# A hybrid attention and mixture-of-experts step: forget bias and masks kept in SBUF tables, and mask and extremum in one VectorE operation

## What is computed

```python
# positions: 16 meta tokens + 256 prompt rows; 8 samples of 16 new rows with 256 cached rows each
z = rms(h, attn_norm) @ w_in                      # split: fox q,k,v, forget logits, diff q,k,v
fq, fk = rms per head of 64; logf = log_sigmoid(ff + b_forget); dq, dk = rope(rms per half head)
c = cumsum(logf)                                  # over positions, per fox head
# group A, 8 fox heads of 64:
s = q.k * 64**-0.5 + c_q - c_k;  s = -inf where k_pos > q_pos;  o = softmax(s) @ v
# group B, 4 diff heads (q1,q2,k1,k2 of 64, v of 128), visible where chunk(k) <= chunk(q), chunks of 64:
p = softmax(q1.k1 * 64**-0.5) - lam * softmax(q2.k2 * 64**-0.5);  o = rms(p @ v) * (1 - 0.2)
h = h + concat(o_fox, o_diff) @ w_out
y = h + moe(rms(h, ffn_norm))                     # top 4 of 32 experts, clamped SwiGLU, gate_up 1024x2048, down 1024x1024
```

## Time and profile before

| | |
|---|---|
| median of 3 runs | 1306.97 us (1306.32 to 1307.01) |
| the profiled execution | 1314.02 us, its span 1312.2 us |
| TensorE busy | 1249.1 us (95%) |
| VectorE, ScalarE, GpSimd busy | 356.9, 197.6, 156.4 us |
| mean granted TensorE clock | 0.957 |
| moved by DMA | 447.05 MB, mean 341 GB/s |
| projections | about 20 to 176 us |
| prompt attention | 177 to 240 us |
| sample attention | 240 to 309 us |
| output projection and router | 309 to 370 us |
| experts | 370 to 1312 us |

### The profile page before, as it was taken

How to read it: one execution, slowest core, us unless ns; L and a number is a source line. 1 busy time by engine, 2 the same in 40 slices (tenths; PEclk the granted TensorE clock), 3 DMA queues, 4 the chain that set the end, 5 groups by cost and what they waited for, 6 DMA issues and landing times.

```text
span 1312.2 us, 16086 instructions
## 1 busy us (share of the span) xinstructions
PE 1249.1 (95%) x6081; PEld 556.6 (42%) x6082; DVE 356.9 (27%) x896; ACT 197.6 (15%) x522; POOL 156.4 (12%) x373
## 2 busy tenths in 40 slices
PE   5799999999989999999999999999999999999997
PEld 3344455664555344343434434343434434343432
DVE  3213335562332142221314222121313212121312
ACT  5111233442411010010101001010101001010100
POOL 0011310220041020202202020201202020210000
PEclk9999975699989999999999999999999999999998
DMA  7912340296049999999999999999999999999994
GB/s 275 338 41 80 117 172 1 81 323 240 22 200 428 429 427 429 429 426 430 428 429 430 427 430 430 427 430 428 429 430 427 430 429 427 430 428 428 428 427 174
DMA packets 54536, 447.05 MB, mean 341 GB/s; under 512 B 10817, under 2 KB 11090, under 8 KB 29922
## 3 DMA queue, kind: packets, MB, share of 16 engines
q1 hardware_dynamic: 54498, 446.54, 82.0%
HBM read 441.66 MB, written 4.86 MB: 340 GB/s over the span
## 4 chain that ended last, share of the span: by engine, by line
PE 65%; DMA 25%; SPq 4%; DVE 2%; POOL 1%; issue 1%; ACT 0%; DVEq 0%; POOLq 0%
DMA arena<-in_w_gate_up 24%; PE psum L1636 17%; PE psum L1604 17%; PE psum L1585 7%; PE psum L1343 6%; PE psum L1507 3%; PE psum L1651 2%; SPq L391 2%; PE psum L1619 1%; PE psum L1615 1%; PE psum L1396 1%; PE psum L1377 1%; PE psum L1426 1%; PE psum L1459 1%; SPq L407 1%
## 5 line engine op out<-in xcount | busy, mean ns | idle before, releaser
L1604 PE MATMUL psum<-arena 128*64 128x512 f32 x2048 | 450.6, 599 | 18.9 <-DMA arena<-in_w_gate_up 18.3
L1604 PEld LDWEIGHTS psum<-arena 128*64 128x64 f32 x2048 | 153.3, 138 | 314.3 <-issue 314.3
L1636 PE MATMUL psum<-arena 128*64 128x512 f32 x1024 | 224.8, 597 | 0.8 <-issue 0.2
L1250 DVE TENSOR_SCALAR arena<-psum 128x256 f32<-128x256 f32 x64 | 26.7, 418 | 432.4 <-PE psum L1604 430.6
L1636 PEld LDWEIGHTS psum<-arena 128*64 128x64 f32 x1024 | 78.8, 138 | 136.1 <-issue 134.7
L1343 PE MATMUL psum<-arena 128*128 128x512 f32 x288 | 127.3, 598 | 0.0
L872 ACT ACTIVATE arena<-arena 128x256 f32<-128x256 f32 x64 | 26.7, 418 | 630.5 <-DVE arena L1250 630.5
L1585 PEld LDWEIGHTS psum<-arena 128*128 128x128 f32 x768 | 88.6, 195 | 16.1 <-issue 16.1
L1585 PE MATMUL psum<-arena 128*128 128x128 f32 x768 | 91.6, 280 | 3.8 <-POOL arena L624 3.8
L617 POOL COPY arena<-arena 128x6 f32 (+1 forms) x16 | 3.0, 188 | 760.0 <-PE psum L1636 703.7
L1651 PE MATMUL psum<-arena 128*128 128x512 f32 x192 | 93.2, 623 | 0.0
(11 more groups left out here) (217 smaller groups left out, 848.9 us busy)
## 6 DMA issues: line engine op xcount, KB each, us to landing
arena<-in_w_gate_up SPq DMA_DIRECT2D x128, 2048.0 KB, 24.9
arena<-in_w_down SPq DMA_DIRECT2D x64, 2048.0 KB, 22.7
arena<-in_w_in SPq DMA_DIRECT2D x6, 2048.0 KB, 20.3
arena<-in_cache_fox_k SPq DMA_DIRECT2D x8, 512.0 KB, 5.7
arena<-in_cache_diff_k SPq DMA_DIRECT2D x8, 512.0 KB, 5.1
arena<-in_cache_fox_v SPq DMA_DIRECT2D x8, 512.0 KB, 5.8
arena<-in_cache_diff_v SPq DMA_DIRECT2D x8, 512.0 KB, 7.1
arena<-in_w_out SPq DMA_DIRECT2D x4, 1024.0 KB, 6.8
```

The source lines that it names most:

```text
L1604: last = mm(banks[n][half], XT[u][:, k, half], piece_slot(s[x])[:, c0:c0 + 512], start=False, stop=(k == 7), skip_group_check=True)
L1636: last = mm(banks[hf][half], actT[:, 4 * i + c, half], w, start=False, stop=(i == 1 and c == 3), skip_group_check=True)
```

## The change

- In the projections, after units 12, 13, 14 and 19, TensorE writes the bias of one pair of heads for all 272 keys to banks 0 and 1 (`keep_table`), and VectorE copies it to two tables in SBUF with the causal mask added where it belongs (`keep_bias`): `T1[p]` for query tile 1, `T0[p]` for query tile 0. GpSimd writes two tables `TD` with the chunk mask for the diff group.
- In the prompt attention the bias matmuls are gone. `maxes` is, for each head, one tensor_tensor_reduce: -(scores + table), written to `probs2` in SBUF, with the minimum of the row as its accumulator output. The exponential reads `probs2` in place, with scale -1.
- `scores(i)` waits for `maxed` in place of `exped`. VectorE's write to `probs2` waits for the transposes of step i - 3.
- The tables lie in ring slot 3. Its first load moves from behind unit 11 to b = 5 of the sample loop.

```diff
--- before.py
+++ after.py
@@ -149,6 +149,9 @@
         probs = [at(a0 + 13696 + 288 * i, 288) for i in range(3)]
         pT = [at3(a0 + 14560 + 384 * i, 3, 128) for i in range(2)]
         probs2 = [at3(5 * PIECE_W + 544 * i, 2, NKEY_P) for i in range(3)]
+        T1 = [at3(3 * PIECE_W + 544 * p, 2, NKEY_P) for p in range(4)]
+        T0 = [at3(3 * PIECE_W + 2176 + 288 * p, 2, META + P) for p in range(4)]
+        TD = [at(3 * PIECE_W + 3328, META + P), at(3 * PIECE_W + 3472, NKEY_P)]
         pT2 = [at3(5 * PIECE_W + 1632 + 768 * i, 2, 384) for i in range(2)]
         assert a0 + 15328 <= 53200
 
@@ -222,6 +225,7 @@
         s_vout = sem("s_vout")
         s_xr, s_wrt, s_bdn, s_bgu = sem("s_xr"), sem("s_wrt"), sem("s_bdn"), sem("s_bgu")
         s_bef, bs_ready = sem("s_bef"), sem("bs_ready")
+        bias_done, bias_kept, chunk_kept = sem("bias_done"), sem("bias_kept"), sem("chunk_kept")
         gates_ready, selg_ready, h_rc = sem("gates_ready"), sem("selg_ready"), sem("h_rc")
         cum_done, ncs_ready, lfT_done = sem("cum_done"), sem("ncs_ready"), sem("lfT_done")
         s_yout = sem("s_yout")
@@ -323,6 +327,14 @@
 
         def S_pair(i):
             return psum[:, 1024 * (i % 2):1024 * (i % 2 + 1)].rearrange("p (a n) -> p a n", a=2)
+
+        TABLE_AT = {12: 0, 13: 1, 14: 2, meta0 + 4: 3}
+        assert [units[u][0] for u in (11, 12)] == [3, 4]
+
+        def masked(x, a):
+            if x["g"] == 1:
+                return TD[x["qt"]]
+            return (T0, T1)[x["qt"]][x["j"]][:, a]
 
         pT_pair = psum[:, 2048:3072].rearrange("p (a n) -> p a n", a=2)
 
@@ -456,7 +468,7 @@
                             sp.dma_start(slot(s).rearrange("p (k n) -> p k n", k=2),
                                          io["w_out"][0, 2 * P * s:2 * P * (s + 1)].rearrange("(k p) n -> p k n", p=P)
                                          ).then_inc(s_wout, 16)
-                    elif bi < 5:
+                    elif bi not in (3, 5):
                         sp.dma_start(piece_slot(bi), piece_src(0, bi - LEAD)).then_inc(ring_in[bi], 16)
 
             for i in range(2):
@@ -473,8 +485,9 @@
                     sp.wait_ge(mixed, NP + 2 * (b - 4) + 2)
                     load_cache(b - 2, "v")
                     load_v3(b - 2)
-                if b == 4:
-                    sp.dma_start(piece_slot(5), piece_src(0, 5 - LEAD)).then_inc(ring_in[5], 16)
+                if b in (4, 5):
+                    s = {4: 5, 5: 3}[b]
+                    sp.dma_start(piece_slot(s), piece_src(0, s - LEAD)).then_inc(ring_in[s], 16)
             sp.wait_ge(scored, NA)
             for t in range(2):
                 sp.dma_start(y[:, t], io["x_prompt"][0, P * t:P * (t + 1), :]).then_inc(s_xr, 16)
@@ -566,6 +579,11 @@
                 nc.gpsimd.tensor_tensor(ov[:, :, 1], ov[:, :, 1], bv[:, :, 1], ALU.add).then_inc(z_out, 1)
 
             g_.wait_ge(zT_copied, upto(is_n, NU))
+            nc.gpsimd.memset(TD[0][:, 0:META], 0.0)
+            nc.gpsimd.memset(TD[1][:, 0:META + P], 0.0)
+            for qt in range(2):
+                last = nc.gpsimd.tensor_copy(TD[qt][:, META + P * qt:META + P * (qt + 1)], C["chunk"])
+            last.then_inc(chunk_kept, 1)
             for i in range(2):
                 g_.wait_ge(s_store[i], 16 * stores_on(NU, i))
             nc.gpsimd.memset(stat[:, 44:45], -0.5)
@@ -759,8 +777,8 @@
                 c = 2 * (i % 3)
                 if x["where"] == "p":
                     for a in range(2):
-                        last = nc.scalar.activation(probs2[i % 3][:, a, 0:x["nk"]], S_pair(i)[:, a, 0:x["nk"]], ACT.Exp,
-                                                    bias=stat[:, 12 + c + a:13 + c + a],
+                        last = nc.scalar.activation(probs2[i % 3][:, a, 0:x["nk"]], probs2[i % 3][:, a, 0:x["nk"]], ACT.Exp,
+                                                    scale=-1.0, bias=stat[:, 12 + c + a:13 + c + a],
                                                     accum_out=stat[:, 18 + c + a:19 + c + a])
                 else:
                     last = nc.scalar.activation(probs[i % 3][:, 0:x["nk"]], banks[i % 2][:, 0:x["nk"]], ACT.Exp,
@@ -954,6 +972,16 @@
                                                 in1=C["maps"][:, 0:1], op0=ALU.mult, op1=ALU.add))
             nc.vector.tensor_scalar(comb, comb, C["maps"][:, 0:1], None, ALU.mult).then_inc(comb_ready, 1)
 
+
+            def keep_bias(p):
+                B = S_pair(0)
+                causal = C["causal"].unsqueeze(1).to_broadcast([P, 2, P])
+                ve.wait_ge(bias_done, p + 1)
+                nc.vector.tensor_copy(T1[p][:, :, 0:META + P], B[:, :, 0:META + P])
+                nc.vector.tensor_tensor(T1[p][:, :, META + P:], B[:, :, META + P:NKEY_P], causal, ALU.add)
+                nc.vector.tensor_copy(T0[p][:, :, 0:META], B[:, :, 0:META])
+                nc.vector.tensor_tensor(T0[p][:, :, META:], B[:, :, META:META + P], causal, ALU.add
+                                        ).then_inc(bias_kept, 1)
 
             for u, (bi, kind, g, t) in enumerate(units):
                 if kind == "v":
@@ -990,6 +1018,8 @@
                 else:
                     ins.then_inc(z_scaled, 1)
                     ve.wait_ge(z_scaled, m + 1)
+                if u in TABLE_AT:
+                    keep_bias(TABLE_AT[u])
                 if m == 1:
                     ve.wait_ge(lfT_done, 1)
                     for t_ in range(4):
@@ -999,6 +1029,9 @@
                     ve.wait_ge(lf_ready, 2)
                     nc.vector.tensor_copy(lf_new[0:META], lf[0:META, 0:1].to_broadcast([META, 8, 8])).then_inc(lf_ready, 1)
 
+
+            keep_bias(3)
+            ve.wait_ge(bias_kept, 4)
 
             def kc_evac(s):
                 ve.wait_ge(kc_T, 2 * s + 1)
@@ -1015,11 +1048,16 @@
                 ve.wait_ge(scored, i + 1)
                 c = 12 + 2 * (i % 3)
                 if x["where"] == "p":
-                    S = S_pair(i)
-                    k0 = META + P * x["qt"]
-                    link(nc.vector.tensor_tensor(S[:, :, k0:k0 + P], S[:, :, k0:k0 + P],
-                                                 C[("causal", "chunk")[x["g"]]].unsqueeze(1).to_broadcast([P, 2, P]), ALU.add))
-                    out_, src = stat[:, c:c + 2], S[:, :, 0:x["nk"]]
+                    if x["g"] == 1:
+                        ve.wait_ge(chunk_kept, 1)
+                    if i >= 3:
+                        ve.wait_ge(turned, i - 2)
+                    for a in range(2):
+                        last = nc.vector.tensor_tensor_reduce(
+                            out=probs2[i % 3][:, a, 0:x["nk"]], in0=S_pair(i)[:, a, 0:x["nk"]], in1=masked(x, a),
+                            scale=-1.0, scalar=3.0e38, op0=ALU.add, op1=ALU.min, accum_out=stat[:, c + a:c + a + 1])
+                    last.then_inc(maxed, 1)
+                    return
                 else:
                     S = banks[i % 2]
                     k0 = META + PAST
@@ -1314,6 +1352,16 @@
                                                zo[upto(is_o, u) % 2][rows_of(u), P * j:P * (j + 1)],
                                                ident[rows_of(u), rows_of(u)])
                 last.then_inc(z_T, 1)
+
+            def keep_table(p):
+                pe.wait_ge(lf_ready, 3)
+                if p >= 1:
+                    pe.wait_ge(bias_kept, p)
+                for a in range(2):
+                    hs = slice(32 * a, 32 * a + 8)
+                    last = mm(S_pair(0)[:, a, 0:NKEY_P], ident[hs, 2 * p + 33 * a:2 * p + 33 * a + 1].to_broadcast([8, P]),
+                              nc_p[hs, 0:NKEY_P], start=True, stop=True)
+                last.then_inc(bias_done, 1)
 
             late = []
             for u, (bi, kind, g, t) in enumerate(units):
@@ -1351,6 +1399,8 @@
                         last = nc.tensor.transpose(banks[6][0:b, 448 + 8 * t_:456 + 8 * t_], ffl[0:8, a:a + b], ident[0:8, 0:8])
                     last.then_inc(lfT_done, 1)
 
+                if u in TABLE_AT:
+                    keep_table(TABLE_AT[u])
                 newest = u - 1 if u < meta0 else -1 if u < meta0 + 4 else meta0 if u < NU - 1 else u
                 while late and late[0] <= newest:
                     turn_z(late.pop(0))
@@ -1380,21 +1430,20 @@
 
             def scores(i):
                 x = att[i]
-                if i >= 2:
+                if i == 0:
+                    pe.wait_ge(bias_kept, 4)
+                elif NP + 2 > i >= 2:
+                    pe.wait_ge(maxed, i - 1)
+                elif i >= 2:
                     pe.wait_ge(exped, i - 1)
                 nk = x["nk"]
                 g = x["g"]
                 if x["where"] == "p":
                     q0, j = P * x["qt"], x["j"]
-                    if g == 0:
-                        for a in range(2):
-                            hs = slice(32 * a, 32 * a + 8)
-                            mm(S_pair(i)[:, a, 0:nk], ident[hs, 2 * j + 33 * a:2 * j + 33 * a + 1].to_broadcast([8, P]),
```

(3 more changed lines are left out.)

## The result

| | before | after |
|---|---|---|
| median of 13 and 13 executions | 1307.67 us | 1301.36 us |
| lowest, highest | 1302.73, 1315.54 | 1295.44, 1310.46 |
| profiled execution, its span | 1314.02, 1312.2 us | 1307.11, 1305.2 us |
| mean granted clock of that execution | 0.957 | 0.970 |

The account below looks back on a forecast made before the run. The prediction took prompt attention as bound by TensorE at half clock. Its terms, -7.5 + 2.1 + 3.4 us with the others 0, summed to -2.0 us, from a median of 1306.97 to 1305.0 us, range 1300.0 to 1310.0.

Parts of the forecast that it names:

- signs of being wrong: Waits on VectorE ahead of prompt attention's transposes, a granted clock above 0.5 there, or a sample stage as long as before.
- What bounds the kernel: Prompt attention, 176.6 to 239.7 us, is bound by TensorE at half clock (0.53 and 0.50).
- the clock comes back earlier: Rival: without the bias, prompt attention might hold full clock, giving 13 us, to 1292; chance 0.06.
- VectorE and ScalarE become the bound: Rival in prompt attention: if a fused operation takes 1.0 us, 8 to 9 us lost, 1313.5; chance 0.07.
- Term 1: Bias matmuls leave the fox steps of prompt attention, all on TensorE's path: -7.5 us.
- Term 2: Four bias products enter the projections, 2.6 us, less a 0.50 us wait for GpSimd at 139.10 that goes: +2.1 us.
- Term 3: VectorE fills the tables during the projections, where it has time, and GpSimd writes the diff masks: 0.
- Term 4: Fused mask and extremum on VectorE in prompt attention, 1.0 us against 1.16 per 272-key step, and exponentials from SBUF: 0.
- Term 5: Moved 2 MB load delays the sample attention's cache loads: waits of 2.1 us for keys, 1.3 for V rows: +3.4 us.
- the wait drops the clock: Rival in the sample attention: waits bring a second half-clock spell of 10.8 us, losing 5.4 us, 1310.4; chance 0.12.
- The sum: All terms over the whole kernel: -7.5 + 2.1 + 3.4 = -2.0 us.
- The rule on transposes: Transposes don't count as busy like matmuls, so removing matmuls among prompt attention's transposes would bring the clock back no sooner.

Follow-up runs that it names:

- dummy_bias: The changed kernel with the bias matmuls put back in every fox step, their result overwritten by the scores; ratio 0.9971 to the kernel before.
- double_bias: The changed kernel with bias matmuls back in every fox step and accumulated into the scores, so the bias counts twice; ratio 0.998 to the kernel before.
- before_products: The kernel before, plus the change's four pairs of bias products in the projections, read by nobody; ratio 1.0002.
- two_ops: The changed kernel with an addition to SBUF and a separate maximum in place of the fused VectorE operation; ratio 1.0036 to the kernel before.
- exped_wait: The changed kernel with scores waiting for the exponentials of step i-2 again, without the earlier release of score banks; 1300.74 us, ratio 0.9951 to the kernel before.
- load_late: The changed kernel with ring slot 3's load issued behind the whole sample attention; 1297.18 us, ratio 0.9924 to the kernel before.
- load_alone: The kernel before, with only the load of ring slot 3 moved into the sample loop; ratio 1.0019.
- fused_alone: The changed kernel without bias tables: only masks in SBUF, bias matmuls accumulated as before, no products in the projections, load still moved; ratio 1.0007 to the kernel before.
- before_pause: The kernel before, with TensorE made to wait, after the scores of step 0, for that step's exponentials; ratio 1.0026.
- before_shift: The kernel before, with five more 128x512 matmuls, results unread, in the projections behind the unit of the last product; ratio 1.0035.

## Why the prediction was right, and where it wasn't

The time was forecast rightly, and partly by luck. The forecast -2.0 us was a sum of work at an unchanged clock. That sum came out at +1.6 ± 0.8 us, and 8.1 us from a higher clock, which the forecast had only as a rival, brought the time to 6.5 us below the kernel before. The signs of being wrong that the prediction named came too: a granted clock above 0.5 in the prompt attention (1.00 for 34 us), and waits ahead of its transposes, for ScalarE at the end of VectorE's chain.

- **What bounds the kernel.** This is the step that failed. "Bound by TensorE at half clock" took the clock of the profile as given. It was so in every profile with TensorE at 0.50 (7.42 us a pair, as forecast), but the changed kernel spends some 25 us less of an execution at 0.50 (0.0096 of mean clock), and at full clock VectorE and ScalarE set the pace, 5.13 us a pair. The rival "the clock comes back earlier", given 0.06, is what happened, and it brought with it the rival "VectorE and ScalarE become the bound", which was priced for operations of 0.8 us or more: they took 0.37 from start to start, but TensorE's work beside the chain had shrunk from 3.5 to 2.06 us. The 13 us (a rounding up of 16 steps at 0.7) were too much for the whole: the clock holds for the fox part and falls in the diff part, and the low stretch then covers more of the sample attention. The whole is worth 8.1 us.
- **Term 1**, -7.5: measured -3.0 ± 1.2 and -3.6 ± 1.3 (dummy_bias, double_bias less the change, at equal clock). The price was right for half clock (9.4 to 7.4 a pair) and wrong for full clock, where 5.79 went to 5.13.
- **Term 2**, +2.1: in the trace it is 2.43 (before_products), and the wait at 139 is gone; by the times it is 2.7 ± 1.0. That the stage ends 2.0 us later in the two profiles says less, since the kernels with the same projections start their prompt attention anywhere from 174.1 to 176.7 us. That something ahead of prompt attention bears on the clock was not foreseen.
- **Term 3**, 0: the start of prompt attention shows no wait on the tables. Right.
- **Term 4**, 0: a step of 272 keys takes 0.81 us for both operations with their read-outs (191.11 to 191.92), forecast 1.0, before 1.16. At half clock it is hidden, as forecast; at full clock it is on the path, and two_ops shows what 1.48 us in its place cost, 4.0 ± 1.2 us. The later wait on VectorE instead of ScalarE, also put at 0, gives about 1 us (exped_wait, 1.1 ± 0.8). The Trainium skill, "VectorE: DVE Perf Modes", "Rules for kernel authors", says to keep the number of operations low rather than to fuse, and by its cost table the four instructions take what the two did, an estimated 1.07 and 1.08 us. The rows differ, 0.81 and 1.16: the measurement decides.
- **Term 5**, +3.4: 2.8 ± 0.8 (the change less load_late) and 3.7 ± 1.0 (load_alone). The size was right and its parts were not. The wait for sample 6's keys came with 2.10 us, forecast 2.1. The 1.3 us for the V rows of sample 4 didn't come: behind the keys' wait no matmul waits for them. The 0.9 us of waits on V rows in the changed kernel are 0.40 at 267.15 and 0.49 at 296.78, where the kernel before waits 0.26 (280.61) and 0.56 us (306.50). In its place stands the rival "the wait drops the clock": it did, for one step, which takes 5.06 us instead of 3.52, 1.5 us more. That is not the spell of 10.8 us that was priced.
- **The sum** at equal clock was -2.0 and is +1.6. Terms: -3.3 for the bias, +2.7, +2.8 to +3.7, -1.0 for the fused operation give +1.2 to +2.1; each is uncertain by about 1 us. Without the clock the change would be a loss.
- **The rule on transposes** ("TensorE: Matmul & The Clock Gate" of the Trainium skill, Part 4). The prediction let it speak against an earlier return of the clock and said that the rows agreed. double_bias and fused_alone turn the same tiles with the same matmuls among them, at clocks that differ; so the share of transposes is not by itself what decides here. No run here varies that share alone.

**What stays open** is what raises the clock. It isn't the removal of the bias matmuls (dummy_bias), the release of the banks (exped_wait), the load (load_alone), a pause (before_pause) or a shift by itself (before_shift). Something ahead of prompt attention gives a part (double_bias against fused_alone). Whether the products do it isn't shown (before_products), and VectorE's work on the tables was never tried without them. The short VectorE operation seems to give another (two_ops loses 0.0071 without it, while fused_alone, 0.0017 ± 0.0025 above before, hardly has it). How these act together wasn't settled.

## What to carry to other kernels

Where a stage runs at half clock, price every edit at both levels and ask which engine is the bound at the other one: what is on the path at half clock (bias matmuls, 9.4 to 7.4 us a pair) may be half hidden at full clock, and what is hidden (VectorE's step) may be the pace. Compare executions at equal mean clock before a gain is put down to work saved. And a prefetch that is displaced did better behind the stage whose DMA engines were already busy than inside it: that alone took this change from 1301 to 1297 us.

## What the runs showed of the hardware

- The mean granted clock differs between kernels of the same matmuls in the stage where it falls (0.9714 and 0.9648), and from run to run of one kernel by 0.014, worth 15 us.
- More idle time of TensorE didn't go with a higher clock: two_ops waits 1.58 us where the change waits 0.91, and has the lower one. In before_pause half clock began 0.5 us behind 2.17 us of waiting.
- The fused operation reads 272 elements from PSUM and 272 from SBUF in 0.37 us from start to start, and its accumulator's read-out of 0.08 us starts with the next operation.
- An issue on SyncE that takes 0.46 us in the kernel before took 3.78 us at 264.86, as the fifth behind the moved load, while the DMA engines were busy throughout; the next one starts only at 268.69.
